# Expert stage of a two-block transformer kernel: residual rows kept in SBUF, three rotating weight buffers in the place of four, a reordered start and end

## The reference

```
def swiglu(x, w_gu, w_down):
    g, u = jnp.split(x @ w_gu, 2, axis=-1)
    return (jax.nn.silu(g) * u) @ w_down

# moe_ffn: each token picks 8 of 64 experts (hidden size 256), with weights w
out = lax.map(expert_block, ...)           # swiglu(x[tok], w_exp_gu[e], w_exp_down[e])
routed = zeros.at[buf_tok].add(out * buf_w)
return routed + swiglu(x2d, w_sh_gu, w_sh_down)     # shared expert

# second_block, end
x = layer_norm_2(DEEPNORM_ALPHA * x + ff, ln3_g[l], ln3_b[l])
```

## Time and profile before

| | us |
|---|---|
| median of 3 runs (lowest to highest) | 2686.91 (2685.09 to 2689.21) |
| the profiled execution's own time | 2685.26 |
| its span | 2683.5 |
| TensorE matmul busy | 2591.7 (97%) |
| VectorE busy | 1973.4 (74%) |
| ScalarE busy | 1408.7 (52%) |
| POOL busy | 274.4 (10%) |

### The profile page before, as it was taken

One profiled execution on the slowest core, in us unless ns is written; L12 is line 12 of the kernel. 1 busy time (PEld: TensorE's weight loads), 2 busy tenths in 40 slices (PEclk: granted clock), 3 DMA queues, 4 the chain that ended last, 5 costly groups with the idle time before them and its releaser, 6 DMA issues.

```text
span 2683.5 us, 34986 instructions
## 1 busy us (share of the span) xinstructions
PE 2591.7 (97%) x12359; PEld 2029.3 (76%) x12359; DVE 1973.4 (74%) x2845; ACT 1408.7 (52%) x2147; POOL 274.4 (10%) x248
## 2 busy tenths in 40 slices
PE   8999999999999999999999998999999999999996
PEld 7878778788887877888887765586667777777773
DVE  4788765677736986777736637456589999999996
ACT  4766652222324546222333233444467789889882
POOL 0000000000000000000001700000026522222210
PEclk9999999999999999999999999999999999999999
DMA  3222232222323133232233551323139999999996
GB/s 112 71 63 70 63 102 94 94 94 94 97 86 102 46 63 67 84 103 94 71 102 119 149 141 28 102 95 129 46 135 363 386 383 387 401 399 395 388 391 277
DMA packets 259959, 435.49 MB, mean 162 GB/s; under 512 B 45374, under 2 KB 199047, under 8 KB 235011
## 3 DMA queue, kind: packets, MB, share of 16 engines
q1 hardware_dynamic: 240931, 395.61, 41.8%
q0 software_dynamic: 18912, 38.36, 4.7%
HBM read 416.44 MB, written 42.62 MB: 171 GB/s over the span
## 4 chain that ended last, share of the span: by engine, by line
PE 82%; DVE 7%; DMA 4%; ACT 3%; issue 3%; POOL 1%; SPq 1%; DVEq 0%; ACTq 0%; POOLq 0%
PE tp L1370 40%; PE tp L2077 4%; PE tp L2079 4%; PE tp L2078 4%; PE tp L1326 2%; PE mp L2099 2%; PE mp L2101 2%; PE mp L2100 2%; PE tp L1476 2%; PE tp L1417 2%; PE tp L1478 2%; PE tp L1477 2%; PE tp L2065 2%; PE tp L1875 1%; DMA arena<-xtab,arena 1%
## 5 line engine op out<-in xcount | busy, mean ns | idle before, releaser
L1370 PE MATMUL tp<-sq_r,arena_r 128*128 128x512 f32 x1056 | 414.3, 392 | 5.8 <-DVE uT_r L2964 3.5
L1370 PE MATMUL tp<-uT_r,arena_r 128*128 128x512 f32 x1056 | 412.0, 390 | 0.0
L1370 PE MATMUL tp<-sq_r,wring_r 128*128 128x512 f32 x1056 | 411.9, 390 | 0.0
L1370 PEld LDWEIGHTS tp<-sq_r,arena_r 128*128 128x128 f32 x1056 | 198.9, 188 | 50.9 <-issue 7.5
L1370 PEld LDWEIGHTS tp<-sq_r,wring_r 128*128 128x128 f32 x1056 | 198.8, 188 | 41.8
L1370 PEld LDWEIGHTS tp<-uT_r,arena_r 128*128 128x128 f32 x1056 | 198.9, 188 | 41.3 <-issue 0.5
L2936 DVE TENSOR_TENSOR wring_r<-wring,arena_r 128x2048 fp32r<-128x2048 f32 x82 | 187.2, 2322 | 48.6 <-ACT arena_r L2228 48.4
L1370 PE MATMUL tp<-arena_r,wring_r 128*128 128x512 f32 x564 | 219.4, 389 | 0.0
L2476 ACT ACTIVATE arena<-arena 128x512 f32<-128x512 f32 x44 | 27.8, 633 | 288.1 <-DVE arena L3022 288.0
L2228 ACT ACTIVATE arena_r<-wring 128x2048 fp32r<-128x2048 f32 x82 | 152.2, 1903 | 39.4 <-DVE arena L3126 11.7
L3877 DVE TENSOR_TENSOR arena_r<-arena,arena_r 128x1024 fp32r<-128x1024 f32 x128 | 150.2, 1212 | 0.7 <-ACT arena_r L2823 0.7
(11 more groups left out here) (631 smaller groups left out, 6134.1 us busy)
## 6 DMA issues: line engine op xcount, KB each, us to landing
wring<-in_w_exp_gu SPq DMA_DIRECT2D x64, 1024.0 KB, 12.2
arena<-in_w_exp_down SPq DMA_DIRECT2D x64, 1024.0 KB, 18.1
uT<-in_w_exp_gu SPq DMA_DIRECT2D x32, 1024.0 KB, 11.6
sq<-in_w_exp_gu SPq DMA_DIRECT2D x32, 1024.0 KB, 11.9
wring<-in_f_up_w SPq DMA_DIRECT2D x22, 1024.0 KB, 5.0
wring<-in_f_up_w SPq DMA_DIRECT2D x44, 512.0 KB, 6.3
wring<-in_f_down_w SPq DMA_DIRECT2D x32, 448.0 KB, 5.4
wring<-in_a_in_proj SPq DMA_DIRECT2D x42, 256.0 KB, 2.7
```

Source lines behind the costliest of these rows:

```text
L1370: ins = nc.tensor.matmul(b[:], parts[wp][:, kk, m * P:(m + 1) * P], xparts[xp][:, kk, :], start=n_k == 0 and q == 0, stop=n_k == k - 1 and ...
```

## The change

The residual rows are taken from PSUM straight to the buffer `wring[0]` and stay there until the adds; the stores to `rest`, its load and ScalarE's wait for the stores are gone. In return the gate/up and down weights rotate through three buffers, and load n is issued once product n-3 is done. The shared down product runs the first half of the activation for four banks ahead of the wait for the second. POOL puts six sets of table entries (in the place of three) ahead of the steps and two sets a step in steps 0 to 8; the table is loaded in step 9 and used from expert 13 on. The loops hold six steps (three on SP). VectorE does the step of expert 63 ahead of the adds of rank 0.

```diff
-        wgu = (flat(uT), flat(sq), wring[SH_GU_SLOT], wring[1 - SH_GU_SLOT])
+        wgu = (flat(uT), flat(sq), wring[SH_GU_SLOT])
-        FIRST, HEAD = 12, 16
+        FIRST, HEAD, LOOP, BUFS = 13, 18, 6, 3
-        rest_rows = rows4(wgu[0])
+        rest_rows = rows4(wring[1 - SH_GU_SLOT][:, :])
 # SP
-            sp.wait_ge(tile_done, RES_TILES)
-            expert_gu(3, 3)
             expert_down(2, 2)
-            expert_down(3, 3)
-            sp.wait_ge(tok_out, SINCE["tok_out"] + 16 * (TC + REST_OUTS))
+            expert_gu(3, 0, 1)
...
-            expert_gu(4, 0, 1)
-            with sp.Fori(0, NE // 4 - 2) as i:
-                for k in range(4):
-                    expert_gu(4 * i + 5 + k, (k + 1) % 4, 4 * i + 2 + k)
-                    expert_down(4 * i + 4 + k, k, 4 * i + 1 + k)
...
+            with sp.Fori(0, (NE - 1) // BUFS - 1) as i:
+                for k in range(BUFS):
+                    expert_gu(BUFS * i + 4 + k, (k + 1) % BUFS, BUFS * i + 2 + k)
+                    expert_down(BUFS * i + 3 + k, k, BUFS * i + 1 + k)
+            expert_down(NE - 1, 0, NE - 3)
...
-                sp.wait_ge(moe["gu"], NE - 3)
-                load_rest()
 # POOL
-            put_entries(range(8, 11))
-            for c in range(TC):
-                pool.wait_ge(tile_evac, RES_TILES + 2 * c + 2)
-                rows = rest[c * P:(c + 1) * P, :]
-                if c < 2:
-                    G.dma_start(rows, ye[c]).then_inc(tok_out, 16)
-                else:
-                    for half in range(2):
-                        G.dma_start(rows[:, 512 * half:512 * half + 512], rest_halves[c][half]).then_inc(tok_out, 16)
+            put_entries(range(8, 14))
...
-                if e < 7:
-                    put_entries(range(11 + 3 * e, 14 + 3 * e))
-                if e == 8:
+                if e < 9:
+                    put_entries(range(14 + 2 * e, 16 + 2 * e))
+                if e + 4 == FIRST:
                     load_table()
 # TensorE
+            def shared_down(m, k):
+                bank = tp[(RES_TILES - NK + m) % NBANK][:]
+                cols_m = slice(m * P, (m + 1) * P)
+                nc.tensor.matmul(bank, shd_hi[:, k, cols_m], sact_hi[k], start=k == 0, stop=False)
+                nc.tensor.matmul(bank, shd_hi[:, k, cols_m], sact_lo[:, k, :], start=False, stop=False)
+                return nc.tensor.matmul(bank, shd_lo[:, k, cols_m], sact_hi[k], start=False, stop=k == 1)
+
+            pe.wait_ge(rt["weights"], 4 + NK + 4)
+            for m in range(NBANK):
+                pe.wait_ge(tile_evac, RES_TILES - NK + m - NBANK + 1)
+                shared_down(m, 0)
             pe.wait_ge(rt["weights"], 4 + NK + 5)
             for m in range(NK):
...
-                if m in (1, 3, 5):
+                if m in (0, 2, 4):
                     m_idx(m // 2, m // 2, m // 2 % 2)
 # ScalarE
-                    take(rest_halves[c][half])
+                    take(rest_rows[:, c, 512 * half:512 * half + 512])
 # VectorE
-                if m in (3, 6):
-                    m_glo(0, 0, 0, (0, 1) if m == 3 else (2,))
-                if m == 7:
-                    m_glo(0, 0, 0, (3,))
+                if m in (1, 3, 6):
+                    m_glo(0, 0, 0, (m // 2 if m < 6 else 2,))
...
+            m_glo(0, 0, 0, (3,))
...
             with dve.Else():
-                add_first_rank()
-                m_step(NE - 1, RING - 1)
+                dve.nop()
+            add_first_rank()
```

More of the change, by code:

```diff
@@ L617, in build @@
         tok_out = sem("tok_out")
-        wg_ready = [sem(f"wg_ready{b}") for b in range(4)]
-        wd_ready = [sem(f"wd_ready{b}") for b in range(4)]
+        wg_ready = [sem(f"wg_ready{b}") for b in range(BUFS)]
+        wd_ready = [sem(f"wd_ready{b}") for b in range(BUFS)]
         moe = {k: sem(f"moe_{k}") for k in (
@@ L2121, in _ @@
             slots.inc()
+            def shared_down(m, k):
[8 more added lines that the diff above has]
+                shared_down(m, 0)
             pe.wait_ge(rt["weights"], 4 + NK + 5)
             for m in range(NK):
[L2124 to L2131 removed]
+                if m >= NBANK:
+                    pe.wait_ge(tile_evac, RES_TILES - NK + m - NBANK + 1)
+                    shared_down(m, 0)
+                shared_down(m, 1).then_inc(tile_done, 1)
                 tiles.inc()
[L2133 removed]
+                if m in (0, 2, 4):
                     m_idx(m // 2, m // 2, m // 2 % 2)
@@ L2146, in _ @@
             for e in range(1, HEAD):
-                m_step(e, e % RING)
-            with pe.Fori(0, (NE - HEAD) // RING - 1) as loop_i:
-                for k in range(RING):
-                    m_step(RING * loop_i + HEAD + k, k)
-            for e in range(NE - RING, NE):
-                m_step(e, e % RING)
+                m_step(e, e % LOOP)
+            with pe.Fori(0, (NE - HEAD) // LOOP) as loop_i:
+                for k in range(LOOP):
+                    m_step(LOOP * loop_i + HEAD + k, k)
+            for e in range(NE - (NE - HEAD) % LOOP, NE):
+                m_step(e, e % LOOP)
             m_actturn(NE - 1)
-            m_down(NE - 1, 1, 3)
+            m_down(NE - 1, 1, (NE - 1) % BUFS)
             crowded = pe.value_load(cnti[0:1, 0:1])
@@ L2884, in _ @@
             for e in range(1, HEAD):
-                m_step(e, e % RING)
-            with act.Fori(0, (NE - HEAD) // RING - 1) as i:
-                for k in range(RING):
-                    m_step(RING * i + HEAD + k, k)
-            for e in range(NE - RING, NE):
-                m_step(e, e % RING)
+                m_step(e, e % LOOP)
+            with act.Fori(0, (NE - HEAD) // LOOP) as i:
+                for k in range(LOOP):
+                    m_step(LOOP * i + HEAD + k, k)
+            for e in range(NE - (NE - HEAD) % LOOP, NE):
+                m_step(e, e % LOOP)
             m_y(NE - 1, 1, (NE - 1) // 2)
@@ L3899, in m_step @@
                     m_xlo(e + 1, (k + 1) % 2)
-                    m_glo(e + 1, (k + 1) % 2, (k + 1) % 4)
-                m_act(e, k % 2, swt[k] if fixed and e < FIRST else cols(table, 4 * e + 2, 1)[0:CAP, :])
-                m_dlo(e, k % 2, k % 4)
+                    m_glo(e + 1, (k + 1) % 2, (k + 1) % BUFS)
+                m_act(e, k % 2, swt[e % RING] if fixed and e < FIRST else cols(table, 4 * e + 2, 1)[0:CAP, :])
+                m_dlo(e, k % 2, k % BUFS)
                 m_actlo(e)
@@ L3932, in _ @@
             for e in range(1, HEAD):
-                m_step(e, e % RING)
-            with dve.Fori(0, (NE - HEAD) // RING - 1) as i:
-                for k in range(RING):
-                    m_step(RING * i + HEAD + k, k)
+                m_step(e, e % LOOP)
+            with dve.Fori(0, (NE - HEAD) // LOOP) as i:
+                for k in range(LOOP):
+                    m_step(LOOP * i + HEAD + k, k)
             added = [0] * TC
@@ L3954, in add_first_rank @@
                     add_rows(c, rank_rows[0])
-            for e in range(NE - RING, NE - 1):
-                m_step(e, e % RING)
+            for e in range(NE - (NE - HEAD) % LOOP, NE):
+                m_step(e, e % LOOP)
             crowded = dve.value_load(cnti[0:1, 0:1])
-            before_first = chain.s
             with dve.If(crowded > CAP):
-                m_step(NE - 1, RING - 1)
                 phase_end(dve, "dve", ph)
@@ L3977, in _ @@
                 phase_end(dve, "dve", ph)
-                add_first_rank()
-            chain.s = before_first
-            added = [0] * TC
             with dve.Else():
-                add_first_rank()
-                m_step(NE - 1, RING - 1)
+                dve.nop()
+            add_first_rank()
             for r in (1, 3):
```

57 lines of the change are left out of this document (19 added, 38 removed).

## The result

The kernel before takes 2688.05 us and the kernel after 2692.52 us (medians of 20 runs each); the ratio of the two is 1.0017, with a 95% interval of 1.0011 to 1.0023. So the change costs 0.17%, where 2682 and a gain were forecast. One run of before took 6703.92 us, which leaves its median where it is; its others lie between 2684.9 and 2691.9, those of after between 2684.3 and 2699.9. The profiled execution of after took 2695.74 us (span 2693.8), 3.2 over its median.

A forecast was written before the change was run, and what follows sets the result against it. TensorE was taken to pace the middle on credit while DMA loads fell behind, and DMA the tail. Head 9.4 gained, 9.5 given back, tail 5.2 gained: 5.1 us, median 2682, range 2669 to 2696.

The forecast's parts named there:

- Shared down product by halves: Start of the experts: half one runs inside TensorE's 3.1 us wait, VectorE's residual adds start earlier; 1.95 us gained.
- Residual rows: Head: residual stores leave POOL's queue and the DMA engines, so TensorE's wait for expert 3's gather goes; 4.1 us gained.
- two stores: Head steps: POOL's cycle falls from 10.9 to 8.4 us, below the 9.8 period, so gathers stop slipping; 4.3 us gained.
- Table from expert 13: Head: table load and the gather from it stall 2.4 us where 1.4 stood; 1.0 us lost, bounds 0 and 2.
- Three buffers: Middle: loads asked for one period later, DMA needs 9.557 us an expert, credit runs out; 9.5 us lost.
- Tail: After the last expert: dropping the residual's read lets the ranks' loads land earlier; 5.2 us gained, bounds 0 and 7.4.
- the head's 9.4 us are given back: Middle: load 63 lands where it does today because DMA sets the pace, cancelling the head's gain by 9.5 us.
- A: Rival for the middle: three buffers are enough and the head's 9.4 us stay; 2672.3 us, chance 0.25.
- C: Rival for the head: no faster, VectorE takes POOL's place and DMA starts late; 2687 to 2690 us, chance 0.1.
- B: Rival for the middle: a shallower queue feeds worse, 15.5 us more over 36 loads; 2697 us, chance 0.2.
- The 435 and 425 GB/s: Middle: the skill's fabric ceiling and measured rate; if 425 were available, loads would outrun TensorE and three buffers would do.
- The second rule: Middle: the skill says DMA engines 7 and 15 usually lag; by it gathers, not queue depth, cause the lag, rate unchanged.

The follow-up runs named there:

- three_only: The kernel before with one edit, three weight buffers instead of four for both gate/up and down weights; 2703.23 us, 1.0053 of before.
- no_down: The kernel after with the experts' down weights loaded only twice and used for all 64, a third of weight bytes left out; 2668.23 us, 0.9925 of before.
- both: The kernel after with four gate/up buffers, three down buffers, residual still in SBUF (placed elsewhere), table from expert 14; 2684.57 us, 0.9989 of before.
- bt_tail: both_turn with the first rank's adds ahead of expert 63 again, the old tail order; 2680.74 us, 0.9973 of before.
- four: The kernel after with four gate/up and four down buffers, residual stored to memory and read back as in before; 2684.27 us, 0.9990 of before.
- wd4: t14 with four buffers for the down weights, gate/up weights staying in three; 2690.15 us, 1.0010 of before.
- t14: The kernel after with the table used from expert 14 instead of 13; 2689.89 us, 1.0009 of before.
- both_turn: both with the turns of expert 0's and 1's rows moved behind the shared down product's last tile and the hT turns; 2682.21 us, 0.9981 of before.
- bt_stores3: both_turn with three table stores a step instead of two; 2688.60 us, 1.0007 of before.
- four14: four with the table used from expert 14 and the two turns moved, residual through memory; 2683.21 us, 0.9984 of before.
- bt_three: bt_again with three gate/up buffers instead of four and nothing else changed; 2690.34 us, 1.0015 of before.
- bt_again: both_turn unchanged, timed once more as a base for others; 2681.49 us, 0.9985 of before.
- nd_stores3: no_down with three table stores a step; 2678.72 us, 0.9970 of before.

## Why the prediction was wrong

Three steps failed. The table's load and the gather behind it were priced at 1.0 us lost and cost 9.2; the shared down product by halves was put at 1.95 gained and lost 1.4; and the price of three buffers, 9.5, was too small: 11.7 in the profile, 14 (8.6 to 20) by the medians of three_only. A gain of 5.1 us became a loss of 4.5.

**The pace before and its cause: right.** TensorE went on credit, and buffers given up shorten it. With transfers of 1 MB the six kernels with three gate/up buffers leave the period of 9.21 at loads 26 to 31, the seven others with four at loads 31 to 51, and before never does; no_down shows that delivery is the cause.

**Its own sum, against the profile.** Forecast 2680.2, measured 2695.74; the median is 3.2 lower, so this account is of a run later than most. Of the 15.5 between, 1.5 were there before the change begins (SP's first load at 2000.43 against 1998.94). The rest are three terms and a small one:

- *Shared down product by halves* (1.95 gained): **failed.** It starts without its wait, but the hT turns start 1.4 later net. Next late was not VectorE's chain of adds but gather 0, at a turn in the midst of the tiles. The bounds (0 to 3.1) left a loss out. 3.4 off. The moved turns bring it back.
- *Residual rows* (4.1) and *two stores* (4.3): **right in size.** Product 2 ends 3.3 later than forecast (2049.2 against 2045.9 with the shift), which is the 3.4 above; products 2 to 9 take 68.7 us against 68.6 forecast, and 72.4 in three_only with its three stores. The cause given for the first, the stores ahead of gather 3, is at best part of it. Three_only has them too, yet product 2 comes 10.2 us after product 1 there (14.3 in before) and no wait stands ahead of the turn; SP asks for the gate/up load of expert 3 at 2030.94, where before does at 2016.95. From issue to landing, gather 3 of before, then of three_only (DMA issues):

```profile
arena<-xtab,arena POOLq DMA_INDIRECT x1, 15.7
```
```profile
arena<-xtab,arena POOLq DMA_INDIRECT x1, 8.4
```

  The third buffer alone takes the wait away, and so does the residual in SBUF with four gate/up buffers (both: 10.1 us from product 1 to 2). In after both are done, so the gain can't be credited to either alone.
- *Table from expert 13* (1.0 lost): **failed, the largest.** The two DMAs in a row were priced too low. The stall is 10.6 where 2.4 was forecast. I took the row of a load and of a gather that landed in 8.2 and 8.1 when the kernel ran late; now the load took 9.7, the gather's issue 4.15, TensorE's slow clock 2 more. 8.2 off, and outside its bounds (0 to 2).
- *Three buffers* (9.5 given back): **too small.** 11.7 between products 12 and 60, 2.2 off by this profile, and more by the medians (below). Of the down weights' ring the forecast has no term.
- *Tail* (5.2): **right in size**, 4.9 (rest 97.6 against 92.7). That the bytes and not the order set it was the forecast's choice of the smaller term; bt_tail shows that the order is worth nothing, and four, with the new order and the residual's read kept, has a rest of 97.2; the kernels with four gate/up buffers and 1 MB of gains in its place lie between (93.8 to 94.7).

Together 1.5 + 3.4 + 8.2 + 2.2 + 0.3 = 15.6.

**By the medians.** Three_only splits the change another way: the three buffers alone cost 0.53%, 14 us (8.6 to 20), where 9.5 were forecast, and all the rest brings 9.7 (give or take 6), where 14.6 were. That is the sign of the result: what the buffers cost is more than what the rest brings.

**What the sum itself had wrong.** These terms were added up as if each reached the end. Across the kernels with four gate/up and three down buffers p12 lies between 2141.1 and 2145.3 and p59 between 2585.0 and 2587.1, without order (transfers of 1 MB); with four of both, p12 is at 2151.3 to 2152.9 and p59 no later for it, at 2585.9 to 2586.7. With three gate/up buffers, p12 between 2140.9 and 2153.2 leads to p60 between 2602.3 and 2605.5; after, with its stall, is at 2610.4, and wd4 at 2609.0 is out of line. So in the profiles a gain in the head reaches the end in part or not at all. The medians agree for the table, of whose 10.6 net 2.6 came through (t14). They don't for the turns (3.6 net, 2.4 through, both_turn) and for the table stores (5.0 net lost in the fastest run, 6.4 to 7.1 in the medians, bt_stores3), and the 9.7 us above are two thirds of a forecast that let everything through. Four14 and both can't decide it, as their down rings differ from what they stand beside. How much of an early gain is given back stays open. I had this mechanism for the forecast's own head ("the head's 9.4 us are given back"), but priced it with one DMA rate, 9.557 us an expert, and let load 63 land where it does today. Measured, the stretch is 9.47 to 9.78 us, and bt_three, whose head is as good as forecast (p12 at 2140.9), still issues load 63 at 2602.3, some 7 us later than a product 63 at 2623 asks for (2623 - 3 x 9.21 = 2595.4). So even without the two failed terms the forecast was, by my estimate from these rows, 6 to 8 us too low.

**The rivals.** A (three do) is out by three_only and bt_three. C (the head no faster) is out: p9 came 7 us earlier net. B (a shallow queue feeds worse, 0.43 us a load) has rows on its side, at a smaller size. The mean of the four windows from 2200 to 2600 is 393 to 394 GB/s in before, four and four14 (four of both buffers), 386 to 391 with four and three (transfers of up to 1 MB), and 380 to 388 with three gate/up buffers, at a DMA share of 1.01 to 1.03 in each. Bt_three against bt_again says 9.73 against 9.55, 0.18 us an expert; the other three-buffer stretches are 9.52 to 9.76. That is one profile each, and no run parts the depth of a ring from the waiting that it brings. Its size as forecast, 15.5 us, is out for bt_three (8.85 in all). The result lies in the range, between the forecast and B, whose own price of 2697 the range left out.

**The rules weighed against the middle term.** The 435 and 425 GB/s weighed there were not to be had: in the stretch the windows show 376 to 395 GB/s in every kernel, and no stretch of 50 us from 2050 on that I read shows more than 405 (four14). The trace's side of that choice held. The second rule, of engines that lag, was tested by no run.

**Open:** how much of the price of a shorter ring is credit and how much slower delivery; what the residual in SBUF is worth by itself; what makes the delivery of one execution 9.5 and of another 9.8 us an expert, perhaps what spreads the runs; and why 2 MB transfers are slower.

**A version that beats both.** bt_tail, 2680.74 us: 0.9973 [0.9963, 0.9983] of before, in eight runs; both_turn and bt_again (0.9981 and 0.9985) can't be told from it. Four gate/up buffers, three down buffers, residual in SBUF, two stores, table from expert 14, turns moved, the tail's old order.

## What to carry to other kernels

When loads fall behind while the engine keeps its pace, the bound is the bytes, whatever engine reads 100% busy. Then ask of each edit whether it moves bytes out or changes how much is asked for ahead, and of every ring that it touches: here the gate/up ring's fourth buffer was worth 8.9 us, and with it in place the waits moved to the down weights' ring. What an edit does to an engine's waits early on may be given back in part; the table's gain was, the turns' came through for the larger part. And a chain through two DMAs (an index table, then the gather from it) has to be priced with the queue that it will meet, not with the one in which its rows were taken.

## What was not expected of the hardware

- One 2 MB transfer in place of two of 1 MB made the stretch 9.78 instead of 9.55 us an expert, 14 us in all; four of 512 KB changed nothing.
- POOL's issue of an indirect DMA takes 0.95 to 5.04 us. In nd_stores3 it is 2 to 3.5 for many in a row, with the DMA engines 69% busy (2000 to 2100), so it is not only a full queue.
- At the same DMA share of 1.01 to 1.03 the engines moved 393 to 394 GB/s in the kernels with four of both buffers and 380 to 388 in those with three gate/up buffers (means of 2200 to 2600).
- After 3.4 and 7.5 us of standing TensorE ran at the lower clock for seven and nine matmuls (0.43 us apart), which added 1.4 to 2 us to each wait.
